# A two-block transformer in split fp32: tiles and attention steps of the second mixers reordered, their scores in three fp32r passes, one transpose of the scan and the heads of the first mixers placed anew

## The reference

```python
def hybrid_mixer(h, ...):            # first block
    proj = h @ w_in                  # q, k, v of three attentions, three gates
    o_a = dsa_attention(...)         # 4 heads, keys chosen by an indexer's top-k
    o_b = moba_attention(...)        # 4 heads
    o_c = diff_attention(...)        # 4 heads, difference of two softmaxes
    merged = sigmoid(ga) * y_a + sigmoid(gb) * y_b + sigmoid(gc) * y_c
    return merged @ w_out

def second_block(...):
    z, xbc, dt_raw, cq, ckv, kr, gates = split_cols(u @ w_in[l], IN_SPLIT_SIZES)
    y_ssd = ssd_branch(...)          # causal convolution of xbc, chunked scan, gate by z
    y_mla = mla_branch(...)          # 8 heads, q and k of 128 + 64 (rotated) columns
    merged = g[..., :D_MODEL] * y_ssd + g[..., D_MODEL:] * y_mla

def causal_block_attention(q, k, v): # in mla_branch
    sc = jnp.einsum('bqhd,bkhd->bhqk', qi, k) * scale
    p = jax.nn.softmax(jnp.where(kpos <= qpos, sc, -inf), axis=-1)
```

## Time and profile before

| | |
|---|---|
| median of three runs | 2669.68 us |
| the profiled execution's own time | 2670.72 us |
| its span, first to last instruction | 2668.9 us |
| TensorE busy | 98% of the span |
| VectorE busy | 68% |
| ACT busy | 56% |
| GpSimd busy | 10% |
| DMA | 471.84 MB, 177 GB/s on average |
| granted TensorE clock | 0.998 of full speed |

### The profile page before, as it was taken

The page is one execution under the profiler, slowest core; times in us unless marked ns, Lnnn a source line. Parts: engine busy times, 40 slices in busy tenths (PEclk is TensorE's granted clock), DMA queues, the critical chain, the costliest instruction groups (busy, mean ns, idle before and its releaser), DMA issues.

```text
span 2668.9 us, 34950 instructions
## 1 busy us (share of the span) xinstructions
PE 2627.0 (98%) x14532; PEld 2245.1 (84%) x14532; DVE 1808.9 (68%) x2207; ACT 1490.6 (56%) x1966; POOL 266.4 (10%) x246
## 2 busy tenths in 40 slices
PE   8999999999999999999999999999999999999999
PEld 7888778888887778888888888888888888888888
DVE  6677766667667766666668587666666686876665
ACT  5456655445456655455457567454554575674543
POOL 0003110000005010000013023100000031131000
PEclk9999999999999999999999999999999999999999
DMA  7555445555555455555555364555555553645553
GB/s 239 197 180 173 142 159 189 189 189 187 191 172 172 142 172 176 190 188 190 189 175 168 108 208 156 189 179 191 182 190 190 177 173 116 198 166 174 182 191 132
DMA packets 342747, 471.84 MB, mean 177 GB/s; under 512 B 18810, under 2 KB 259516, under 8 KB 342588
## 3 DMA queue, kind: packets, MB, share of 16 engines
q1 hardware_dynamic: 342588, 469.61, 53.2%
HBM read 468.46 MB, written 1.11 MB: 176 GB/s over the span
## 4 chain that ended last, share of the span: by engine, by line
PE 87%; DVE 7%; ACT 4%; issue 1%; POOL 0%; DMA 0%; SPq 0%; DVEq 0%; ACTq 0%
PE PS L100 84%; DVE WL L109 3%; PE PS L103 2%; ACT WH L106 1%; DVE XB L117 1%; DVE RL L117 1%; POOL XB L109 0%; ACT RH L106 0%; DMA ST<-in_ffn_w_gate 0%; ACT SB L106 0%; DVE SB L120 0%; ACT L106 0%; ACT JK L106 0%; DVE ZR L117 0%; SPq L142 0%
## 5 line engine op out<-in xcount | busy, mean ns | idle before, releaser
L109 DVE TENSOR_TENSOR WL<-ST,WH 128x2048 fp32r<-128x2048 f32 (+3 forms) x442 | 1012.1, 2290 | 360.1 <-ACT WH L106 358.8
L100 PE MATMUL PS<-XHL,WH 128*128 128x512 f32 (+1 forms) x4096 | 1123.2, 362 | 3.1 <-DVE GS L109 2.3
L106 ACT ACTIVATE WH<-ST 128x2048 fp32r<-128x2048 f32 (+3 forms) x442 | 830.2, 1879 | 151.5 <-PE PS L100 133.9
L100 PEld LDWEIGHTS PS<-XHL,WL 128*128 128x128 f32 x3456 | 652.8, 189 | 124.7
L100 PE MATMUL PS<-XHL,WL 128*128 128x256 f32 x3456 | 735.5, 279 | 0.0
L100 PEld LDWEIGHTS PS<-XHL,WH 128*128 128x128 f32 x4096 | 634.8, 190 | 12.7 <-issue 3.2
L100 PE MATMUL PS<-WH,XHL 128*128 128x512 f32 (+3 forms) x1472 | 463.7, 389 | 0.0
L100 PE MATMUL PS<-WH,RH 128*128 128x512 f32 (+1 forms) x1056 | 410.6, 389 | 13.9 <-DVE QB L114 6.1
L100 PE MATMUL PS<-WL,RH 128*128 128x512 f32 (+1 forms) x1056 | 407.9, 386 | 0.0
L100 PE MATMUL PS<-WH,RL 128*128 128x512 f32 (+1 forms) x1056 | 407.6, 386 | 0.0
L100 PEld LDWEIGHTS PS<-WH,XHL 128*128 128x128 f32 x1472 | 275.2, 189 | 59.2 <-issue 7.0
(11 more groups left out here) (235 smaller groups left out, 1927.2 us busy)
## 6 DMA issues: line engine op xcount, KB each, us to landing
ST<-in_ffn_w SPq DMA_DIRECT2D x132, 1024.0 KB, 5.0
ST<-in_w_in SPq DMA_DIRECT2D x106, 1024.0 KB, 5.1
ST<-in_ffn_w_down SPq DMA_DIRECT2D x44, 1024.0 KB, 4.9
ST<-in_ffn_w_gate SPq DMA_DIRECT2D x43, 1024.0 KB, 5.1
ST<-in_ffn_w_up SPq DMA_DIRECT2D x43, 1024.0 KB, 5.1
ST<-in_w_ssd_out SPq DMA_DIRECT2D x16, 1024.0 KB, 5.0
ST<-in_w_branch SPq DMA_DIRECT2D x8, 1024.0 KB, 5.0
ST<-in_w_out SPq DMA_DIRECT2D x8, 1024.0 KB, 5.0
```

The lines of the kernel that those rows point to most:

```text
L100: return self.eng.matmul(o, l, r, start=start, stop=stop) if self.eng else Said()
L106: return self.eng.activation(o, v, f, **kw) if self.eng else Said()
L109: return self.eng.tensor_tensor(o, a, b, op) if self.eng else Said()
```

## The change

Four parts; the values are computed as before but for the rounding of the scores.

1. `MIX2`, the order of the second mixers' tiles. One `xbc` tile instead of three comes ahead of the query tiles, the first `gate2` pair stands between the first two `uq` tiles, `ukv` and `uq` alternate, all `xbc` tiles come before the `mla` tiles. The steps of the four pairs of heads get new places, most of them further apart. `z` 6 and 7 take banks 6 and 7 alone.
2. The scores. `QNT`, `KNT` and `QRT` become fp32r; VectorE writes their low parts into `QBL`, `KVL`, `KRL` (over `QB`, `KV`, `KRS`, which have been transposed by then), and each fp32 matmul becomes three fp32r matmuls. The copy of `QRT` moves from VectorE to ACT.
3. The scan. `gb` moves from behind the tile of its step to before it; `gated` 5, 6 and 7 move one step later.
4. The first mixers. A table `HEADS1` places each head's steps, `TURNED` and `FT_AT` the transposes: `sc` of `b` 1 goes from step 12 to 11, `av` of `b` 0 from before tile 13 to behind tile 12, `tn` of `b` 1 from before to behind tile 14, `kc` from behind tile 14 to before tile 15, `tn` of `c` 1 from before tile 18 to behind 17, `av` of `c` 0 and `c` 1 behind tile 18, `av` of `a` 1 from before to behind tile 24.

```diff
-MIX2 = [("xbc", 0), ("xbc", 1), ("xbc", 2), ("uq", 0), ("uq", 1), ("uq", 2), ("ukv", 0), ("ukv", 1), ("uq", 3),
...
+MIX2 = [("xbc", 0), ("uq", 0), ("gate2", 0), ("uq", 1), ("uq", 2), ("ukv", 0), ("uq", 3), ("ukv", 1), ("xbc", 1),
...
+HEADS1 = [("b", 0, 10, (11, 0), (12, 0), (12, 1)), ("b", 1, 11, (13, 0), (14, 1), (15, 0)),
+          ("c", 0, 15, (16, 0), (17, 0), (18, 1)), ("c", 1, 16, (17, 0), (17, 1), (18, 1)),
+          ("c", 2, 17, (18, 0), (19, 0), (20, 0)), ("c", 3, 18, (19, 0), (20, 0), (21, 0)),
+          ("a", 0, 20, (21, 0), (22, 0), (23, 0)), ("a", 1, 21, (22, 0), (23, 0), (24, 1))]
+TURNED = [("qc", 0, (12, 0)), ("qc", 2, (12, 0)), ("kc", 0, (15, 0)), ("kc", 2, (15, 0))]
+FT_AT = (23, 1)
...
-    for p, (a, b, c, d) in enumerate((((15, 0), (16, 0), (17, 0), (18, 0)), ((16, 1), (17, 1), (18, 1), (19, 1)),
-                                      ((19, 0), (20, 0), (21, 0), (22, 0)), ((20, 1), (21, 1), (22, 1), (23, 1)))):
+    for p, (a, b, c, d) in enumerate((((14, 1), (16, 0), (17, 1), (19, 0)), ((17, 0), (18, 0), (19, 0), (21, 0)),
+                                      ((19, 1), (21, 0), (22, 1), (23, 1)), ((21, 1), (22, 1), (24, 0), (25, 0)))):
...
-        add(s, 1, "gb", g, 1)
+        add(s, 0, "gb", g, 1)
...
-    for n, s in enumerate((32, 33, 35, 36, 39, 40, 41, 42)):
+    for n, s in enumerate((32, 33, 35, 36, 39, 41, 42, 43)):
...
-            banks = (min(range(4, 8), key=lambda b: last[b]),)
+            banks = (min(range(6 if key in (("z", 6), ("z", 7)) else 4, 8), key=lambda b: last[b]),)
...
-                b, r = banks[h], slice(64 * h, 64 * h + 64)
                 for t, (a, c) in enumerate(TILES):
-                    kk = slice(0, 128 * (t + 1))
-                    e.matmul(PS[:, b, c], QNT[:, i2, h, a], KNT[i2][:, h, kk], True, False)
-                    m = e.matmul(PS[:, b, c], QRT[r, i2, 0, a], QRT[r, i2, 1, kk], False, True)
...
+                    e.matmul(o, qn[:, h, a], kn[:, h, 0:128 * (t + 1)], t == 0, False)
+                    e.matmul(o, ql[:, t, :], kn[:, h, 0:128 * (t + 1)], False, False)
+                    e.matmul(o2, qn[:, h, a], kl[:, 0:t + 1, :], False, False)
...
+                for h in range(2):
+                    r = slice(64 * h, 64 * h + 64)
+                    e.matmul(PS[:, banks[h], c], qr[r, a], kr[r, kk], False, False)
+                for h in range(2):
+                    r = slice(64 * h, 64 * h + 64)
+                    e.matmul(PS[:, banks[h], c], ql[r, t, :], kr[r, kk], False, False)
...
+            e.activation(QRT[:, i2], PS[:, banks[2], :].rearrange("p (h t) -> p h t", h=2), ACT.Copy).then_inc(*e.done("qt", p, key, 2))
...
-            e.tensor_copy(QRT[:, key % 2], PS[:, banks[2], :].rearrange("p (h t) -> p h t", h=2)).then_inc(*e.done("qt", p, key, 2))
...
+            e.tensor_tensor(ql, PS[:, banks[0], :].rearrange(four, h=2, t=2),
+                            QNT[:, i2].bitcast(F32).rearrange("p h (t c) -> p h t c", t=2), ALU.subtract).then_inc(*e.done("ql", p, key, 0))
...
+            for h in range(2):
+                e.stt(KVL[:, :, 2 * key + h, 0:128], PS[:, banks[1], 256 * h:256 * h + 256].rearrange("p (t c) -> p t c", t=2),
...
+            for q, o in enumerate((QBL[:, :, key, 128:256], kr)):
+                e.tensor_tensor(o, PS[:, banks[2], q * 256:q * 256 + 256].rearrange("p (t c) -> p t c", t=2),
```

More of the change, by code:

```diff
@@ L33 @@
 GATE_AT = {i: FFN.index(("g", i)) for i in range(NP)}
[L34 to L37 removed]
+MIX2 = [("xbc", 0), ("uq", 0), ("gate2", 0), ("uq", 1), ("uq", 2), ("ukv", 0), ("uq", 3), ("ukv", 1), ("xbc", 1),
+        ("xbc", 2), ("gate2", 1), ("xbc", 3), ("xbc", 4), ("xbc", 5), ("xbc", 6), ("xbc", 7), ("xbc", 8), ("xbc", 9),
+        ("xbc", 10), ("xbc", 11), ("mla", 0), ("mla", 1), ("z", 0), ("z", 1), ("z", 2), ("gate1", 0), ("z", 3),
+        ("gate1", 1), ("z", 4), ("z", 5), ("z", 6), ("z", 7)]
 FFN_POOL, MIX1_POOL, MIX2_POOL = (), (), ()
@@ L201, in mix1_steps @@
     add(11, 1, "hm", "kc")
[L202 to L205, removed]
+    for name, c, s in TURNED:
+        add(*s, "tr", (name, c), 1)
     n, m, had = 0, 0, []
-    for kind, x, s in (("b", 0, 10), ("b", 1, 12), ("c", 0, 15), ("c", 1, 16), ("c", 2, 17), ("c", 3, 18), ("a", 0, 20),
-                       ("a", 1, 21)):
+    for kind, x, s, nm, tn, av in HEADS1:
         k = 1 if kind == "c" else 2
@@ L217, in mix1_steps @@
         add(s, 1, "ex", (kind, x), 0, bufs)
-        add(s + 1, 0, "nm", (kind, x), 0, bufs)
-        add(s + 2, 0, "tn", (kind, x), k, bufs)
-        add(s + 3, 0, "av", (kind, x), 1, bufs)
+        add(*nm, "nm", (kind, x), 0, bufs)
+        add(*tn, "tn", (kind, x), k, bufs)
+        add(*av, "av", (kind, x), 1, bufs)
         n, m = n + 2, m + k
@@ L226, in mix1_steps @@
     for h in range(4):
-        add(23, 1, "ft", h, 1)
+        add(*FT_AT, "ft", h, 1)
     for j in range(6):
@@ L425, in build @@
     CB = ar("CB", [128, 2, 2, 260], 80896)
-    QNT, QRT = sb("QNT", [128, 2, 2, T], F32, R2), sb("QRT", [128, 2, 2, T], F32, R2 + 16384)
-    KNT = [sb(f"KNT{i}", [128, 2, T], F32, R2 + 4096 + 16384 * i)[:, :, :] for i in range(2)]
+    QNT, QRT = sb("QNT", [128, 2, 2, T], F32R, R2), sb("QRT", [128, 2, 2, T], F32R, R2 + 16384)
+    KNT = [sb(f"KNT{i}", [128, 2, T], F32R, R2 + 4096 + 16384 * i)[:, :, :] for i in range(2)]
+    QBL, KVL = ar("QBL", [128, 2, 4, 384], A0, F32R), ar("KVL", [128, 2, 8, 256], A0 + 12288, F32R)
+    KRL = ar("KRL", [128, 2, 8, 64], A0 + 28672, F32R)
     TMPH = [sb(f"TMP{i}", [128, 2, T], F32, R2 + 6144 + 16384 * i)[:, :, :] for i in range(2)]
@@ L1993, in vector_task2 @@
         elif what == "tq":
[L1994 to L1998, removed]
-            e.tensor_copy(QRT[:, key % 2], PS[:, banks[2], :].rearrange("p (h t) -> p h t", h=2)).then_inc(*e.done("qt", p, key, 2))
+            i2, four = key % 2, "p (h t c) -> p h t c"
+            ql = QBL[:, :, key, :].rearrange("p t (a c) -> p t a c", c=128)[:, :, 0:3:2, :].rearrange("p t h c -> p h t c")
+            kr = KRL[:, :, 2 * key:2 * key + 2, :].rearrange("p t h d -> p t (h d)")
+            e.wait_ge(*at("qt", p, key, 0))
+            e.tensor_tensor(ql, PS[:, banks[0], :].rearrange(four, h=2, t=2),
+                            QNT[:, i2].bitcast(F32).rearrange("p h (t c) -> p h t c", t=2), ALU.subtract).then_inc(*e.done("ql", p, key, 0))
+            e.wait_ge(*at("qt", p, key, 1))
+            for h in range(2):
+                e.stt(KVL[:, :, 2 * key + h, 0:128], PS[:, banks[1], 256 * h:256 * h + 256].rearrange("p (t c) -> p t c", t=2),
+                      GKQ[:, l:l + 1], KNT[i2][:, h, :].bitcast(F32).rearrange("p (t c) -> p t c", t=2), ALU.mult,
+                      ALU.subtract).then_inc(*e.done("ql", p, key, 1) if h else e.done())
+            e.wait_ge(*at("qt", p, key, 2))
+            for q, o in enumerate((QBL[:, :, key, 128:256], kr)):
+                e.tensor_tensor(o, PS[:, banks[2], q * 256:q * 256 + 256].rearrange("p (t c) -> p t c", t=2),
+                                QRT[:, i2, q, :].bitcast(F32).rearrange("p (t c) -> p t c", t=2),
+                                ALU.subtract).then_inc(*e.done("ql", p, key, 2) if q else e.done())
         elif what == "sc":
```

19 lines of the change are left out of this document (15 added, 4 removed).

## The result

The changed kernel takes 2624.93 us (median of 4 runs, 2624.07 to 2626.32) against 2669.64 us for the kernel before on the same chip: 44.7 us less, a ratio of 0.9833 (95% interval 0.982 to 0.9845). The forecast was 2625. The profiled execution took 2626.32 us, its span is 2624.5 us.

The account below looks back on a forecast made before the run. TensorE, busy 98% of the span, bounds the kernel. Gains of 17.9 us per second and 4.6 per first mixer, twice both, make 45.0 off 2670.72; less 1.04 for the median gives 2624.7, rounded to 2625 us; range 2613 to 2646.

Parts of the forecast that it names:

- opening (part 1): Second mixers, steps 4 to 10: the new tile order removes most TensorE waits on VectorE, 5.6 us a mixer.
- attention's waits (part 1): Second mixers' attention: steps placed further apart remove most of 3.6 us of TensorE waits, gain 2.0 us a mixer.
- scores (part 2): Second mixers: fp32r scores take 2.4 us a pair instead of 4.07, gain 6.7 us a mixer.
- scan (part 3): Second mixers' scan: four `gs` waits, 2.6 us, and the step 45 wait, 1.0, go; 3.6 us a mixer.
- first mixer (part 4): First mixers: 4.3 us around tile 12 and 0.4 at `av` of a 1, less 0.1; 4.6 us a mixer.
- the rival of slow narrow matmuls: Scores: fp32r at 128 columns costs 0.21 us, so 4.1 us a pair and no gain; 2638 us, chance 18%.
- Hidden while VectorE stays below TensorE: Second mixers' steps 4 to 28: VectorE's extra 1.7 us a pair, 6.7 a mixer, costs no time.
- VectorE lags: Rival, attention: low parts and waits for ACT and GpSimd make `tn` 2 us late each pair; 16 us, 2641, chance 18%.
- The change lets more of these coincide: Attention: more VectorE splits meet a GpSimd add; one split so took 2.37 us against 1.73 alone.
- the 14 us a mixer: Second mixers: eleven GpSimd adds of 1.3 us beside splits could cost VectorE up to some 14 us.
- The slower rival: Attention: TensorE stands for the whole VectorE chain, 6.8 us for each of 8 pairs, 54 us; 2679, chance 3%.
- I price that at nothing: Scan: the moved transpose of B needs a bank that `hy` frees about then; priced at no cost.

Follow-up runs that it names:

- e9: The kernel before with only the new order of the second mixers' tiles and the banks of `z` 6 and 7; 2657.96 us.
- e4: The kernel before with part 1 alone, tile order and new places of the attention steps; 2650.98 us.
- e2: The changed kernel without part 2, scores again in fp32 matmuls; 2636.44 us.
- e10: The changed kernel with the queries' low part written twice in each `tq`, 0.7 us more VectorE a pair; 2628.81 us.
- e7: The changed kernel with the queries' low part written four times in each `tq`, 2.2 us more VectorE a pair; 2643.13 us.
- e8: The changed kernel with the attention steps of the four pairs in their old places, new tile order kept; 2644.00 us.
- e5: The changed kernel with part 3 undone: transpose of B behind the tile again, `gated` 5 to 7 a step sooner; 2632.45 us.
- e6: The changed kernel with the rotated half of the scores written head by head instead of the two heads in turn; 2628.39 us.
- e1: The kernel before with part 2 alone, scores in fp32r with low parts on VectorE; 2660.63 us.

## Why the prediction was right, and where only its sum was

By its own steps, us a mixer:

| term | forecast | measured | by |
|---|---|---|---|
| opening (part 1) | 5.6 | 6.1 | e9, without the `gs` wait |
| attention's waits (part 1) | 2.0 | 2.9 | e4 against e9, likewise |
| scores (part 2) | 6.7 | 6.15, 5.9 | changed against e2 |
| scan (part 3) | 3.6 | 2.6 | e2 against e4 |
| second mixer | 17.9 | 17.95, 17.5 | |
| first mixer (part 4) | 4.6 | 4.7, 4.6 | |

- **The opening.** Right in kind and nearly in size: the waits for `cv1` and the query eviction are gone. Of the small ones that I left (1.1), 0.8 stands.
- **Attention.** The sum was short by 0.9 for part 1 alone. Of the 1.6 us of waits that I left, 0.7 stands with the order and places alone (e4, before the first `tq`); 0.7 and 0.9 came with the low parts, before `tn` of pair 1, where I had counted no slack. The table books these to the scores. Attention and scores together were forecast at 8.7 and measured at 9.0 and 8.8.
- **Scores.** 2.45 us a pair against my 2.4. The 128-row half took 1.56 and not 1.3 + 0.2, the rotated half 0.89 against 0.9, which is 0.57 of the 128-row half where I had taken 0.67. The 128-column fp32r matmul costs 0.11 us, near the row that I had taken it from, and the rival of slow narrow matmuls is out. The term fell short by the 0.7 to 0.9 us of waits that its VectorE work brings.
- **"Hidden while VectorE stays below TensorE"** was the step that failed, though it cost the sum little. It argued from a load of 134 in 177 us. e10 and e7 show that 0.7 us more a pair already costs 3.9 and 2.2 us costs 18.2. What decides is the chain from `tq` through the low parts, the minima and the softmax to `tn`, with splits between. The rival "VectorE lags" priced this at 16 us for 2 us a pair; e7 measured 18.2 for 2.2, 15.9 by the stages. What did not come true is its condition, probabilities 2 us late for each pair: the change stops just short of it.
- **GpSimd beside VectorE** cost nothing more than before. The groups of VectorE's splits in steps 4 to 28 of the changed kernel (by form: count, busy us, mean ns, idle before):

```profile
L109 DVE TENSOR_TENSOR WL<-ST,WH 128x2048 fp32r<-128x2048 f32 x22 | 51.4, 2338 | 3.5 <-ACT WH L106 3.5
L109 DVE TENSOR_TENSOR WL<-ST,WH 128x1536 fp32r<-128x1536 f32 x4 | 7.0, 1752 | 0.6 <-ACT WH L106 0.6
```

  In the kernel before the same 26 splits took a mean of 2370 and 2053 ns, 1.9 us more in all. "The change lets more of these coincide" had the sign wrong. A split that begins under a running GpSimd add of 1.3 us is longer by up to 0.8 us, an add that begins under a split is long itself and costs VectorE nothing; first a split in the kernel before, then both cases in the changed one:

```profile
1502.39 3.06 DVE L109 TENSOR_TENSOR WL<-ST,WH 128x2048 fp32r<-128x2048 f32 x1
1534.61 1.29 POOL L109 TENSOR_TENSOR XB<-XB,TMP 128x512 f32<-128x512 f32 x1 [4.79 <-DVE XB L117]
1535.17 2.87 DVE L109 TENSOR_TENSOR WL<-ST,WH 128x2048 fp32r<-128x2048 f32 x1
1540.63 3.21 POOL L109 TENSOR_TENSOR XB<-XB,TMP 128x512 f32<-128x512 f32 x1 [4.73 <-DVE XB L117]
```

  In steps 4 to 28 the kernel before has four splits of the first kind, the changed one has one. The rule that I cited from the Trainium skill, SBUF — State Buffer, Who interferes with whom, agrees with these rows; the 14 us a mixer that I made of it did not come.
- **The slower rival** had its place right and its name wrong. TensorE does stand for VectorE's low parts where no tile lies between, but at the bank of `tq`, not at the scores, and not pair by pair: 19.1 us (e8), some 5 of it, by my estimate of 1.6 each, by the lower clock behind three waits. With the old places the whole change would still have been faster, by some 26 us.
- **Scan.** "I price that at nothing" was wrong by 1.3 us a mixer, and the term by 1.0: the transposes before the tile wait for banks that `hy`'s readers on VectorE free behind a split, and with the part undone (e5) these waits shrink from 1.2 to 0.6 and the one behind tile 37 goes. That they came because small tasks take their banks in turn is likely, but no run tests it. Against that, up to 1.7 us a mixer of late loads is absorbed (e5, layer 0).
- **The first mixers.** As forecast, both at tile 12 (12.1 us became 7.1, with 0.9 of scores gone to tile 11) and at `av` of a 1.
- **The range.** Its ends are not what its terms add to: 2625 less 5.6 and 5 is 2614, where the text has 2613, and half of both larger rivals gives 2640, where it has 2646. Nothing hangs on it.

That the total came out within 0.1 us is luck: the interval of the medians is far wider, and the term for part 1 was 1.5 a mixer too small while those for scan and scores were 1.0 and 0.6 to 0.8 too large. Alone the parts are worth 18.3 (1), 8.7 (2) and 7.8 to 9.3 (4). Part 3 was measured only by taking it out, since in the old tile order its earlier copy would write over `CB` while the last convolution still reads it; it stays open what it is worth alone.

## What to carry to other kernels

Move steps and shrink work together: shorter matmuls without new places gave two thirds of their worth, and the new places without the low parts a third of theirs. Before adding work to an engine whose average load is low, follow the chain that passes through it from one consumer's start to the next, and list which buffers its output now holds longer; a bank that is freed by a second reader is a new wait, even where the data are in time. Read the granted clock behind every wait too, since it can add as much as the wait. When a remaining wait of 0.5 us tempts, look first at what stands behind the instruction that would then wait.

## What the runs showed of the hardware

- Matmuls on rows 0 to 63 and 64 to 127 overlap even when six of one half precede six of the other in the program (1.17 us against 0.89 for alternate ones, where twelve of 128 rows took 1.56), and then start out of the program's order (e6, 1468.916 before 1469.019).
- fp32r at 128 columns costs 0.11 us a matmul with new weights each time, against 0.12 at 256 columns: the half as wide matmul is hardly cheaper, while an fp32 matmul of 128 columns takes two starts of 0.20 to 0.21.
- After a wait of 1.3 us the clock was down for most of a tile and cost 1.7 us (e1, layer 0); a wait of 1.1 us at the same place in layer 1 cost nothing more. In e8 the same wait of 1.97 us was followed by a clock of 0.56 in one layer and of 1.00 in the other, the one of 3.74 us by 0.53 and 0.51. What decides it stays open.
- Whether a GpSimd add beside a VectorE split costs VectorE time went by which began first (3.06 and 2.87 us instead of 2.29 under an add of 1.29; 2.29 where the add, then 3.21 us long, began second).
- The first 190 us of the program differ by up to 2.8 us between executions of equal code, everything later far less. The six executions that show a lowered clock at 24 to 29 us (0.66 in the kernel before and the changed one) took 189.9 to 190.9 us, the eight without it 188.2 to 190.0.
